# Mixing stage of the first block: the short tile of sparse attention moved into the first long tile, the second long tile turned over two PSUM banks

## The chip, the cores and the metric

The kernel runs on one core of one Trainium2 chip. The metric is the device time of one execution in microseconds (us); lower is better. The median of three runs is 3070.9 us (3065.38 to 3075.09).

## What is computed

A first block of two layers over 272 tokens (16 meta tokens and 256 of the sequence) of width 1024, then a second block of two layers. The change is in the first block. Each of its layers begins with one projection of the tokens and two mixers on its columns:

```
proj = h @ w_in[l]
dq, dk, dv, dz, db, da, sq, sk, sv, iq, ik, iw = split(proj)
o_dn = deltanet_group(dq, dk, dv, dz, db, da, ...)        # gated delta rule, 4 heads
o_sa = dsa_group(sq, sk, sv, iq, ik, iw, ..., k_top=64)   # sparse attention, 8 heads of 64
mix  = concatenate([o_dn, o_sa]) @ w_out[l]
```

In the sparse attention an index score (Relu of 8 products of iq and ik, weighted by iw) picks the 64 best earlier tokens of each token; the attention is a softmax over those alone:

```
score  = sum_h relu(qi . ki / 8) * wi ;  sel = top_k(score, 64)
logits = q . k[sel] / 8, masked where sel > position
out    = softmax(logits) @ v[sel]
```

The first 16 tokens have no more than 16 earlier ones, so all are taken and no ranking is needed.

## The kernel before

The 272 tokens lie in three tiles, TILES = (0, 16), (16, 128), (144, 128); below they are the short, the first long and the second long tile, c = 0, 1, 2. The mixing stage (mixers) has three parts that share the engines: projections (35 products n = 0 to 34, each of 16 TensorE instructions, most of 128 x 272), delta_rule and sparse_attention. Each part gives each engine a generator. A generator yields a due time and then issues the instructions of one step; together() always takes the generator with the smallest due time. The due times are plain numbers without a unit that the engine sees: they fix the order in which an engine's instructions are put, once, when the program is built, and nothing more. An engine works through that order and stops at any semaphore that is not yet there.

The steps that matter here:

- projection_time(n): due time of projection n. Projections 0 to 11 feed the convolution of the delta rule, 12 to 14 its gates, 15 the index key (ik), 16 to 19 iq, 20 to 23 sq, 24 to 27 sk, 28 to 30 the values sv (7 us each), 31 to 34 the output gate z. Results are copied out of PSUM by ScalarE (L267 to L276). A rotated copy for the rope goes through four DMAs (swap, L206), then VectorE (L311 to L316).
- on_tensor of projections first turns the layer's parameters (L224), which six small loads bring (L168), and then starts projection 0 (L247), which waits for three loads made ahead (load_ahead, L119).
- Ranking, RANK_START: for each long tile and head an index product (L707) on TensorE, a Relu (L757) on ScalarE and an accumulation (L802, L804) on VectorE, with two banks and two buffers, so that product h waits for Relu h-2 and Relu h for accumulation h-2. Then eight rounds of maximum and replace (L814, L816).
- Attention, ATTEND_ORDER = (1, 2, 0) at ATTEND_START = (116, 157, 198): logits (L724) head by head, scaled and masked by VectorE (L838), row maximum (L841), exponential (L766), reciprocal (L847), scaling (L773). Then for each head: turn of the probabilities into bank 6 (L735), copy to SBUF in one instruction for each of the c + 1 key tiles (L783), product with the values (L743). At the end of a tile one copy into mixT (L787).
- The delta rule goes over the three tiles too: steps gcum/gc, kv, kk, LA, then levels v with products LX (L450), YP (L457) and PY (L460) and subtractions on VectorE (L645, L648), then wu (L465, L467), wS (L474) and oS (L479 to L482). At due time 177 it closes with squares (L508), a product with ones (L408), logarithms (L511) and an exponential (L513).
- mix_and_route follows: its first product (L991) reads all of mixT.

Of the kernel before, what the change touches and what calls it, by code (L numbers as in the profile page):

```python
# [9 lines left out]
ALU = mybir.AluOpType  # L10
# [3 lines left out]
P = 128  # L14
# [119 lines left out]

def projections(nc, m, l, A, S):
# [196 lines left out]
def delta_rule(nc, m, S, ctx):  # L332
# [182 lines left out]
    def chunk_on_scalar(act, c, t0, n):  # L515
# [23 lines left out]
        if c == 2:  # L539
            yield end_time(c, 4)  # L540
# [124 lines left out]
RANK_START = {1: 80.0, 2: 98.0}  # L665
ATTEND_ORDER = (1, 2, 0)
ATTEND_START = (116.0, 157.0, 198.0)


def sparse_attention(nc, m, S, ctx):  # L670
# [12 lines left out]
    den = sb("s_den", [P, NH])  # L683

# [4 lines left out]
    RANKED = [t0 + n > TOP_K for t0, n in TILES]  # L689
    assert RANKED == [False, True, True]  # L690

    def half(h):
        return slice(64 * (h % 2), 64 * (h % 2) + 64)

    def on_tensor(pe):
# [13 lines left out]
        for a, c in enumerate(ATTEND_ORDER):  # L709
            t0, n = TILES[c]  # L710
            ns = t0 + n
            at = ATTEND_START[a]
            for h in range(NH):
# [5 lines left out]
                if h < 2 and a:  # L719
                    pe.wait_ge(S["s_pT_sb"], a * NH)  # L720
                    pe.wait_ge(S["s_out"], a)
                if h >= 2:
                    pe.wait_ge(S["s_logit_sb"], q - 1)
                nc.tensor.matmul(ps[6 + h % 2][0:n, 0:ns], m.sqT[half(h), h // 2, t0:t0 + n], m.skT[half(h), h // 2, 0:ns],  # L724
                                 start=True, stop=True).then_inc(S["s_logit"], 1)
            for h in range(NH):
# [4 lines left out]
                if h:  # L731
                    pe.wait_ge(S["s_pT_sb"], q)
                for j in range(c + 1):
                    s0, w = TILES[j]
                    mm = nc.tensor.transpose(ps[6][0:w, j * P:j * P + n], lg[0:n, h, s0:s0 + w], m.ident[0:n, 0:n])  # L735
                mm.then_inc(S["s_pT"], 1)
                yield at + 24.5 + 2.2 * h
                if q == 0:
                    pe.wait_ge(S["proj_by_act"], 12 + 13 + 3)
                pe.wait_ge(S["s_pT_sb"], q + 1)  # L740
# [6 lines left out]
    def on_scalar(act):  # L747
# [10 lines left out]
        for a, c in enumerate(ATTEND_ORDER):  # L758
            t0, n = TILES[c]
            ns = t0 + n  # L760
            at = ATTEND_START[a]
# [2088 lines left out]
```

## Time and profile before

| | |
|---|---|
| median of 3 runs | 3070.9 us (3065.38 to 3075.09) |
| profiled execution, its time | 3067.97 us |
| its span, first to last instruction | 3065.9 us |
| TensorE busy, matmuls | 2507.4 us, 82% of the span |
| VectorE busy | 856.7 us, 28% |
| ScalarE busy | 572.3 us, 19% |
| TensorE clock granted, mean | 0.878 |

The span is 2.1 us shorter than the profiled execution's own time. Rows of the trace are read as follows. PE is TensorE's matmuls, PEld its weight loads, DVE VectorE, ACT ScalarE, SPq the queue that issues the DMAs. A row of the timeline has the start, the duration, the engine, the line of the kernel, the operation with its result and its inputs, the shape and how many instructions are merged in it; in brackets how long the engine was idle before it and what ended that. A row of the windows has the stretch and its length, then busy time and count for PE, PEld, DVE, ACT and POOL, then the granted TensorE clock (1.00 is 2.4 GHz, 0.50 is 1.2 GHz), the share of the DMA engines' time and GB/s. A row of the groups has busy time and mean duration in ns, then the idle time before. Both layers run the same instructions; rows of the first stand for both where nothing else is said.

### The profile page before, as it was taken

What the parts mean: (1) busy time and instruction counts of PE and PEld (TensorE: products, weight loads), DVE (VectorE), ACT (ScalarE), POOL (GpSimd) and SP (SyncE); (2) the same over time, 40 slices, a digit from 0 to 9 for tenths busy, and PEclk for the clock granted to TensorE, in tenths of its full rate; (3) what the DMA queues carried; (4) which work ended last, traced back from release to release, by engine and by line L of the source; (5) the groups of instructions that cost most, each with busy time, mean ns of one, the idle gap of its engine ahead of it and who ended that gap; (6) DMA issues with size and microseconds to landing.
All of it is one profiled execution on the core that took longest, in us unless ns stands there. A gap on an engine that the chain in (4) does not pass through costs nothing. (4 is left out here: it accounts for less than half of the span.)

```text
span 3065.9 us, 32692 instructions
## 1 busy us (share of the span) xinstructions
PE 2507.4 (82%) x12088; PEld 1844.6 (60%) x12088; DVE 856.7 (28%) x2016; ACT 572.3 (19%) x1323; POOL 0.2 (0%) x4
## 2 busy tenths in 40 slices
PE   6888768786989668874787888989979778798998
PEld 5665544335766454432655567778867556687886
DVE  2472043223473042223112352111110324411111
ACT  1214120102213210012112222011010223301110
POOL 0000000000000000000000000000000000000000
PEclk9999769998889669997898688999989868899999
DMA  5120319992220218993633002533244220233331
GB/s 184 65 70 28 136 41 396 399 393 79 85 70 28 110 55 336 408 399 128 183 117 110 1 1 83 184 118 137 109 112 154 64 82 1 77 116 137 137 137 41
DMA packets 162921, 422.16 MB, mean 138 GB/s; under 512 B 40306, under 2 KB 54108, under 8 KB 138220
## 3 DMA queue, kind: packets, MB, share of 16 engines
q1 hardware_dynamic: 162796, 420.56, 37.4%
q8 instruction: 71, 1.16, 0.2%
q14 instruction: 54, 0.44, 0.0%
HBM read 414.82 MB, written 1.05 MB: 136 GB/s over the span
## 5 line engine op out<-in xcount | busy, mean ns | idle before, releaser
L2611 PE MATMUL bank<-hT,W 128*128 128x256 f32 x1024 | 229.5, 385 | 19.1 <-DVE hT L1603 11.9
L2619 PE MATMUL bank<-u_hid,W 128*128 128x256 f32 x1024 | 225.2, 381 | 19.2 <-ACTq L2633 19.2
L247 PE MATMUL bank<-hT,W 128*128 128x272 f32 x928 | 237.8, 414 | 0.0
L2611 PEld LDWEIGHTS bank<-hT,W 128*128 128x128 f32 x1024 | 196.2, 193 | 52.3 <-issue 25.4
L2619 PEld LDWEIGHTS bank<-u_hid,W 128*128 128x128 f32 x1024 | 193.2, 190 | 51.1 <-issue 25.5
L247 PEld LDWEIGHTS bank<-hT,W 128*128 128x128 f32 x928 | 184.9, 202 | 44.0 <-issue 4.3
L1230 PE MATMUL bank<-W,e_hs 128*32 128x512 f32 x1024 | 138.4, 701 | 60.2 <-DMA W<-in_w 58.5
L2644 DVE TENSOR_TENSOR xT<-xT,bank 128x256 f32<-128x256 f32 x128 | 53.9, 421 | 428.7 <-PE bank L2619 428.7
L1209 PE MATMUL bank<-e_sel,rowsH 128*128 128x128 f32 (+1 forms) x768 | 149.2, 328 | 19.3 <-DVEq L1317 11.6
L1209 PEld LDWEIGHTS bank<-e_sel,rowsH 128*128 128x128 f32 (+1 forms) x768 | 113.9, 204 | 62.8 <-issue 25.3
L2521 PE MATMUL bank<-hT,W 128*128 128x256 f32 x512 | 122.1, 394 | 20.0 <-PEq L2473 18.3
L1230 PEld LDWEIGHTS bank<-W,e_hs 128*32 128x32 f32 x1024 | 40.4, 126 | 157.0 <-issue 157.0
L2521 PEld LDWEIGHTS bank<-hT,W 128*128 128x128 f32 x512 | 101.0, 199 | 38.5 <-issue 23.8
L1772 PE MATMUL bank<-hT,W 128*128 128x256 f32 (+1 forms) x544 | 121.9, 384 | 2.3 <-issue 2.1
L1772 PEld LDWEIGHTS bank<-hT,W 128*128 128x128 f32 (+1 forms) x544 | 99.8, 185 | 24.0 <-issue 8.9
L2630 ACT ACTIVATE u_rel<-bank 128x256 f32<-128x256 f32 x64 | 24.5, 383 | 402.1 <-PE bank L2611 402.1
L1220 PE MATMUL bank<-e_back,e_y 128*128 128x272 f32 x288 | 83.7, 413 | 18.9 <-DVE yT L1336 13.1
L2434 PE MATMUL bank<-hT,W 128*128 128x256 f32 x256 | 77.7, 470 | 3.5 <-DVEq L2454 3.5
L1220 PEld LDWEIGHTS bank<-e_back,e_y 128*128 128x128 f32 x288 | 45.6, 188 | 52.7 <-DVE yT L1336 45.1
L2434 PEld LDWEIGHTS bank<-hT,W 128*128 128x128 f32 x256 | 60.8, 244 | 18.1 <-DVEq L2454 3.9
L1336 DVE TENSOR_TENSOR yT<-yT,bank 128x272 f32<-128x272 f32 x144 | 61.6, 437 | 33.6 <-PE bank L1220 29.6
L991 PE MATMUL bank<-mixT,W 128*128 128x272 f32 x256 | 64.9, 418 | 1.7 <-PEq L875 1.1
(535 smaller groups left out, 3332.5 us busy)
## 6 DMA issues: line engine op xcount, KB each, us to landing
W<-in_w SPq DMA_DIRECT2D x128, 1024.0 KB, 10.2
W<-in_w_in SPq DMA_DIRECT2D x41, 2048.0 KB, 9.0
e_Wd<-in_w SPq DMA_DIRECT2D x64, 1024.0 KB, 10.3
W<-in_w_up SPq DMA_DIRECT2D x16, 2048.0 KB, 9.0
W<-in_w_down SPq DMA_DIRECT2D x16, 2048.0 KB, 7.9
W<-in_w_out SPq DMA_DIRECT2D x8, 2048.0 KB, 8.4
W<-in_cmp_w SPq DMA_DIRECT2D x4, 2048.0 KB, 8.7
W<-in_mem_w_kv SPq DMA_DIRECT2D x4, 2048.0 KB, 8.1
```

Source lines behind the costliest of these rows:

```text
L247: mm = nc.tensor.matmul(bank[:, 0:T], w[:, k, c0:c0 + P], m.hT[:, k, :], **st)
L991: mm = nc.tensor.matmul(ps[n % 4][:, 0:T], w[:, k, n % 4 * P:n % 4 * P + P], m.mixT[:, k, :], start=(k == 0), stop=(k == KT - 1))
L1209: mm = nc.tensor.matmul(o, m.rowsH[0:nt, c, d * P:(d + 1) * P], sel[0:nt, c, :], start=(c == 0), stop=(c == 2))
L1220: nc.tensor.matmul(ps[6 + d % 2][:, 0:T], y[:, d * P:(d + 1) * P], back[:, 0, :], start=True, stop=True).then_inc(S["e_part"], 1)
L1230: mm = nc.tensor.matmul(ps[2][32 * j:32 * j + 32, :], hs[:, k, 32 * j:32 * j + 32], Wu[:, j, :, k, :], start=(k == 0), stop=(k == KT - 1))
L1336: nc.vector.tensor_tensor(m.yT[:, d, :], m.yT[:, d, :], ps[6 + d % 2][:, 0:T], ALU.add).then_inc(S["e_y_free"], 1)
L1772: mm = nc.tensor.matmul(o, wv[:, k, a:a + w], m.hT[:, k, :], **st)
L2434: mm = nc.tensor.matmul(bank[:, 0:S2], wm[:, k, n % 4 * P:n % 4 * P + P], m.hT[:, k, :], start=(k == 0), stop=(k == KT - 1))
L2521: mm = nc.tensor.matmul(ps[q % 2][:, 0:S2], wm[:, k, n % 4 * P:n % 4 * P + P], m.hT[:, k, :], start=(k == 0), stop=(k == KT - 1))
L2611: mm = nc.tensor.matmul(ps[j % 2][:, 0:S2], wa[:, k, j * P:(j + 1) * P], m.hT[:, k, :], start=(k == 0), stop=(k == KT - 1))
L2619: mm = nc.tensor.matmul(ps[4 + n % 2][:, 0:S2], wb[:, k, n * P:(n + 1) * P], hid[:, x, k, :], start=(k == 0), stop=(k == 3))
L2644: nc.vector.tensor_tensor(m.xT[:, n, :], m.xT[:, n, :], ps[4 + n % 2][:, 0:S2], ALU.add).then_inc(S["u_y_free"], 1)
```

## The change

1. The short tile leaves the third place of ATTEND_ORDER. Its work for all eight heads is done in one piece inside the first long tile: logits into banks 6 and 7 after that tile's logits, mask, maximum and subtraction on VectorE, one exponential on ScalarE, sum and division on VectorE, eight turns into bank 6, one copy, eight products, one copy into mixT.
2. The second long tile turns its heads alternately into banks 6 and 0.
3. A head's copies out of the turn bank (one for each key tile) become one instruction over all key tiles and all 128 partitions.
4. The turn of the parameters goes behind projections 0 and 1.
5. Due times: projections 20 and up, RANK_START of the second long tile 98 to 92, ATTEND_START 116 to 120 and 157 to 161, the gate's Silu.

```diff
@@ projection_time
+    if n < 20:
+        return 54.0 + 4.0 * (n - 15)
     if n < 28:
-        return 54.0 + 4.0 * (n - 15)
+        return 75.0 + 5.0 * (n - 20)
     if n < 31:
-        return 112.0 + 12.0 * (n - 28)
-    return 148.0 + 5.0 * (n - 31)
+        return 122.0 + 8.0 * (n - 28)
+    return 146.0 + 6.0 * (n - 31)
@@ projections, on_tensor
-        yield 0
-        pe.wait_ge(S["params_loaded"], 16 * 6)
-        nc.tensor.transpose(ps[7][:, 0:81], m.prm[0:81, :], m.ident[0:81, 0:81]).then_inc(S["params_turned"], 1)
...
         for n, (kind, chunk, c0, idx) in enumerate(plan):
+            if n == 2:
+                pe.wait_ge(S["params_loaded"], 16 * 6)
+                nc.tensor.transpose(ps[7][:, 0:81], m.prm[0:81, :], m.ident[0:81, 0:81]).then_inc(S["params_turned"], 1)
@@ delta_rule, chunk_on_scalar
-            yield end_time(c, 4)
+            yield max(end_time(c, 4), projection_time(34) + 4)
@@ sparse_attention
-RANK_START = {1: 80.0, 2: 98.0}
-ATTEND_ORDER = (1, 2, 0)
-ATTEND_START = (116.0, 157.0, 198.0)
+RANK_START = {1: 80.0, 2: 92.0}
+ATTEND_START = {1: 120.0, 2: 161.0}
...
+    def turn_bank(a, h):
+
+        return ps[0] if a and h % 2 else ps[6]
@@ sparse_attention, on_tensor
+            if a == 0:
+                yield at + 9.5
+                pe.wait_ge(S["s_logit_sb"], NH)
+                for h in range(NH):
+                    mm = nc.tensor.matmul(ps[6 + h % 2][0:M, h // 2 * M:h // 2 * M + M], m.sqT[half(h), h // 2, 0:M], m.skT[half(h), h // 2, 0:M], start=True, stop=True)
+                mm.then_inc(S["s_short_logit"], 1)
+                yield at + 17
+                pe.wait_ge(S["s_short_prob"], 1)
+                for h in range(NH):
+                    mm = nc.tensor.transpose(ps[6][0:M, M * h:M * h + M], short[:, 0, h, :], m.ident[0:M, 0:M])
+                mm.then_inc(S["s_short_pT"], 1)
+                yield at + 19
+                pe.wait_ge(S["proj_by_act"], 12 + 13 + 1)
+                pe.wait_ge(S["s_short_pT_sb"], 1)
+                for h in range(NH):
+                    mm = nc.tensor.matmul(ps[7][half(h), h // 2 * M:h // 2 * M + M], m.sv[0:M, 0, h * 64:(h + 1) * 64], short[:, 1, h, :], start=True, stop=True)
+                mm.then_inc(S["s_short_pv"], 1)
             for h in range(NH):
                 q = a * NH + h
                 yield at + 23 + 2.2 * h
                 if h == 0:
                     pe.wait_ge(S["s_prob"], a + 1)
-                if h:
+                if a == 0 and h:
                     pe.wait_ge(S["s_pT_sb"], q)
+                if a and h == 1:
+                    pe.wait_ge(S["proj_by_act"], 12 + 13 + 3 + 4)
+                if a and h >= 2:
+                    pe.wait_ge(S["s_pT_sb"], q - 1)
                 for j in range(c + 1):
                     s0, w = TILES[j]
-                    mm = nc.tensor.transpose(ps[6][0:w, j * P:j * P + n], lg[0:n, h, s0:s0 + w], m.ident[0:n, 0:n])
+                    mm = nc.tensor.transpose(turn_bank(a, h)[0:w, j * P:j * P + n], lg[0:n, h, s0:s0 + w], m.ident[0:n, 0:n])
                 mm.then_inc(S["s_pT"], 1)
                 yield at + 24.5 + 2.2 * h
@@ sparse_attention, on_scalar
+                if a == 0 and h == 4:
+                    act.wait_ge(S["s_short_in"], 1)
+                    nc.scalar.activation(short[:, 0, :, :], short[:, 0, :, :], ACT.Exp).then_inc(S["s_short_exp"], 1)
...
-                for j in range(c + 1):
-                    w = TILES[j][1]
-                    i = nc.scalar.activation(pT[0:w, h % 2, j, 0:n], ps[6][0:w, j * P:j * P + n], ACT.Copy)
-                i.then_inc(S["s_pT_sb"], 1)
-            yield at + 41.5
+                nc.scalar.activation(pT[:, h % 2, 0:c + 1, 0:n], turn_bank(a, h)[:, 0:(c + 1) * P].rearrange("p (j t) -> p j t", j=c + 1)[:, :, 0:n],
+                                     ACT.Copy).then_inc(S["s_pT_sb"], 1)
+            yield at + 42
```

On ScalarE the copy of the turned probabilities of the short tile stands behind scaling 1 of the first long tile and its copy into mixT behind scaling 6. On VectorE the short tile's mask and maximum are due at 132, its sum and division at 135.5, both between steps of the first long tile.

## Rows read from the trace of the kernel before

**Rows 1.** The page, part 1: busy time, share of the span, instructions.

```profile
PE 2507.4 (82%) x12088; PEld 1844.6 (60%) x12088; DVE 856.7 (28%) x2016; ACT 572.3 (19%) x1323; POOL 0.2 (0%) x4
```

**Rows 2.** The windows, whole core, three of the first layer's.

```profile
160.00:190.00 30.00, 28.11 (x158) 21.91 (x156) 23.40 (x52) 6.54 (x17) 0.00 (x0) 1.00 0.13 47
...
205.00:220.00 15.00, 8.88 (x46) 7.06 (x46) 11.22 (x31) 1.19 (x2) 0.00 (x0) 0.77 0.00 0
...
333.00:347.00 14.00, 5.40 (x41) 3.78 (x39) 1.66 (x12) 5.73 (x33) 0.00 (x0) 0.50 0.00 0
```

**Rows 3.** The timeline, end of the first layer's mixing stage.

```profile
306.93 0.81 PE L735 MATMUL bank<-k_ident,W 128*16 128x128 f32 x3 [4.71 <-ACTq L774]
307.77 0.58 ACT L783 ACTIVATE W<-bank 16x128 f32<-16x128 f32 x3 [0.92 <-PE bank L735]
...
308.40 1.73 PE L743 MATMUL bank<-W,sv 16*64 16x128 f32 x6 [0.67 <-ACT W L783]
...
332.13 0.60 ACT L787 ACTIVATE mixT<-bank 128x512 f32<-128x512 f32 x1 [1.81 <-PE bank L743]
...
346.89 17.10 PE L991 MATMUL bank<-mixT,W 128*128 128x272 f32 x64 [0.57 <-PEq L875]
...
364.25 14.91 PE L991 MATMUL bank<-mixT,W 128*128 128x272 f32 x64 [0.26 <-issue]
```

**Rows 4.** The groups by shape, 306 to 333 us.

```profile
L783 ACT ACTIVATE W<-bank 128x128 f32<-128x128 f32 x16 | 3.2, 249 | 0.0
```

**Rows 5.** The timeline from the last delta product to the scalings.

```profile
290.37 1.06 PE L482 MATMUL bank<-d,d 128*128 128x128 f32 x8
...
292.40 0.51 ACT L766 ACTIVATE W<-W,s_mx 128x272 f32<-128x272 f32 x1
...
297.69 1.37 ACT L508 ACTIVATE d_sq<-d_oT 128x272 f32<-128x272 f32 x4
...
304.09 1.11 ACT L513 ACTIVATE d_sq<-d_sq 128x1088 f32<-128x1088 f32 x1
...
305.11 1.74 ACT L773 ACTIVATE W<-W,s_den 128x272 f32<-128x272 f32 x4
```

**Rows 6.** The timeline and DMA issues, start of both layers' stages.

```profile
12.29 4.94 SPq L119 DMA_DIRECT2D W<-in_w_in  x1
...
32.68 0.40 PE L224 MATMUL bank<-k_ident,prm 81*128 81x81 f32 x1 [10.31 <-DMA prm<-in_ln_b]
...
W<-in_w_in SPq DMA_DIRECT2D x1, 2048.0 KB, 19.8
...
725.30 0.07 DVE L1502 MEMSET xT<- 128x9 f32 x1 [11.92 <-issue]
...
728.67 0.40 PE L224 MATMUL bank<-k_ident,prm 81*128 81x81 f32 x1 [23.35 <-DMA prm<-in_ln_b]
```

**Rows 7.** The timeline, ranking and delta levels, engine by engine.

```profile
156.51 5.62 PE L247 MATMUL bank<-hT,W 128*128 128x272 f32 x16
...
194.50 7.04 PE L242 MATMUL bank<-W,hT 128*16 128x512 f32 x16
...
211.98 0.84 PE L724 MATMUL bank<-skT,sqT 64*128 64x144 f32 x2 [5.14 <-DVE W L838]
...
229.84 1.95 PE L450 MATMUL bank<-d,d 128*128 128x128 f32 x16
...
163.06 0.69 DVE L645 TENSOR_TENSOR d<-d,bank 128x512 f32<-128x512 f32 x1 [4.12 <-PE bank L457]
...
179.78 0.36 DVE L802 TENSOR_SCALAR s_score<-W,bai 128x272 f32<-128x272 f32 x1
...
180.26 0.40 ACT L757 ACTIVATE W<-bank 128x272 f32<-128x272 f32 x1 [4.79 <-DVEq L805]
...
119.79 2.41 SPq L206 DMA_DIRECT2D xT<-iqT  x4
...
124.60 1.29 DVE L311 TENSOR_TENSOR xT<-xT,k_sin 128x1088 f32<-128x1088 f32 x1 [0.89 <-DMA xT<-iqT]
```

More of the change, by code:

```diff
@@ L683, in sparse_attention @@
     den = sb("s_den", [P, NH])
+    M = N_META
+    short = sb("s_short", [M, 2, NH, M])
+    short_bias = sb("s_short_bias", [M, M])
+    short_mx = sb("s_short_mx", [M, 2, NH])
     room, at = m.W[:, SLOTS - 1, :], NH * T
@@ L688, in sparse_attention @@
     pT = room[:, at + 2 * T:at + 2 * T + 6 * P].rearrange("p (h j t) -> p h j t", h=2, j=3)
-    RANKED = [t0 + n > TOP_K for t0, n in TILES]
-    assert RANKED == [False, True, True]
+    assert TILES[0] == (0, M) and M <= TOP_K
     def half(h):
         return slice(64 * (h % 2), 64 * (h % 2) + 64)
+    def turn_bank(a, h):
+        return ps[0] if a and h % 2 else ps[6]
     def on_tensor(pe):
@@ L708, in on_tensor @@
                                  start=True, stop=True).then_inc(S["s_idx"], 1)
-        for a, c in enumerate(ATTEND_ORDER):
+        for c in (1, 2):
             t0, n = TILES[c]
             ns = t0 + n
-            at = ATTEND_START[a]
+            at = ATTEND_START[c]
+            a = c - 1
             for h in range(NH):
@@ L739, in on_tensor @@
                     pe.wait_ge(S["proj_by_act"], 12 + 13 + 3)
+                    pe.wait_ge(S["s_short_out"], 1)
                 pe.wait_ge(S["s_pT_sb"], q + 1)
@@ L757, in on_scalar @@
                 nc.scalar.activation(rel[0:n, h % 2, 0:ns], ps[6 + h % 2][0:n, 0:ns], ACT.Relu, scale=0.125).then_inc(S["s_rel"], 1)
-        for a, c in enumerate(ATTEND_ORDER):
+        for c in (1, 2):
             t0, n = TILES[c]
             ns = t0 + n
-            at = ATTEND_START[a]
+            at = ATTEND_START[c]
+            a = c - 1
             yield at + 11
@@ L773, in on_scalar @@
                 nc.scalar.activation(lg[0:n, h, 0:ns], lg[0:n, h, 0:ns], ACT.Copy, scale=den[0:n, h:h + 1])
+                if a == 0 and h == 1:
+                    act.wait_ge(S["s_short_pT"], 1)
+                    nc.scalar.activation(short[:, 1, :, :], ps[6][0:M, 0:NH * M].rearrange("s (h t) -> s h t", h=NH), ACT.Copy).then_inc(S["s_short_pT_sb"], 1)
+                if a == 0 and h == 6:
+                    act.wait_ge(S["s_short_pv"], 1)
+                    nc.scalar.activation(m.mixT[:, 4:8, 0:M], ps[7][:, 0:4 * M].rearrange("p (h t) -> p h t", h=4), ACT.Copy).then_inc(S["s_short_out"], 1)
             act.drain().then_inc(S["s_prob"], 1)
@@ L822, in on_vector @@
             dve.drain()
-        for a, c in enumerate(ATTEND_ORDER):
+        yield ATTEND_START[1] - 1
+        nc.vector.tensor_scalar(short_bias[:, :], m.causal[0:M, 0, 0:M], -1.0, BIG, ALU.add, ALU.mult)
+        dve.drain()
+        for c in (1, 2):
             t0, n = TILES[c]
             ns = t0 + n
-            at = ATTEND_START[a]
-            mask = bias[0:n, c - 1 if RANKED[c] else 0, 0:ns]
-            if not RANKED[c]:
-                yield at
-                nc.vector.tensor_scalar(mask, m.causal[0:n, c, 0:ns], -1.0, BIG, ALU.add, ALU.mult)
-                dve.drain()
+            at = ATTEND_START[c]
+            a = c - 1
+            mask = bias[0:n, a, 0:ns]
             for h in range(NH):
@@ L844, in on_vector @@
             dve.drain().then_inc(S["s_max"], 1)
+            if a == 0:
+                yield at + 12
+                dve.wait_ge(S["s_short_logit"], 1)
+                w = short[:, 0, :, :]
+                for y in range(2):
+                    nc.vector.scalar_tensor_tensor(w[:, y:NH:2, :], ps[6 + y][0:M, 0:NH // 2 * M].rearrange("s (h t) -> s h t", h=NH // 2), 0.125,
+                                                   short_bias[:, :].unsqueeze(1).to_broadcast([M, NH // 2, M]), ALU.mult, ALU.add)
+                dve.drain()
+                nc.vector.tensor_reduce(short_mx[:, 0, :], w, AX.X, ALU.max)
+                dve.drain()
+                nc.vector.tensor_tensor(w, w, short_mx[:, 0, :].unsqueeze(2).to_broadcast([M, NH, M]), ALU.subtract)
+                dve.drain().then_inc(S["s_short_in"], 1)
+                yield at + 15.5
+                dve.wait_ge(S["s_short_exp"], 1)
+                nc.vector.tensor_reduce(short_mx[:, 1, :], w, AX.X, ALU.add)
+                dve.drain()
+                nc.vector.reciprocal(short_mx[:, 1, :], short_mx[:, 1, :])
+                dve.drain()
+                nc.vector.tensor_tensor(w, w, short_mx[:, 1, :].unsqueeze(2).to_broadcast([M, NH, M]), ALU.mult)
+                dve.drain().then_inc(S["s_short_prob"], 1)
             yield at + 17
```

13 lines of the change are left out of this document (7 added, 6 removed).

## The prediction

> **What bounds the kernel now.** The page's first part says TensorE is busy for 82% of the span [rows 1]. That average hides the stage this change is in: the mixing stage, which runs once a layer, from 32.7 to 346.9 us and again from 728.7 us. The windows show its two halves. The first is crowded: from 160 to 190 us TensorE is busy 28.1 of 30 us at full clock, and the hole is from 205 to 220 us, 8.9 busy of 15 us at a granted clock of 0.77. The end is a chain with little beside it: from 333 to 347 us TensorE is busy 5.4 of 14 us at a granted clock of 0.50, which is 1.2 GHz [rows 2]. The timeline of that end shows the second long tile's eight heads one after another from 306.93 us to the tile's output copy at 332.13 us, 3.15 us each, then the short tile alone, and only at 346.89 us the output projection (L991), which needs all of mixT [rows 3]. So I read the change as: take the short tile off the end, and pay for it in the crowded part.
>
> **The end of the stage: what is removed.** The second tile's output copy ends at 332.73 us and L991 starts at 346.89 us [rows 3]. No more of that than the 0.57 us that L991's row has as idle before it is the handover, which stays. I take 13.8 us as gone in each of the two layers (bounds 13.6 and 14.2).
>
> **The turns over two banks.** One head costs 0.84 us to the first copy, 0.58 us of copies, 0.05 us of wait, and the rest of its 3.15 us, 1.7 us, is products; TensorE idles 0.67 us for the copies [rows 3]. The diff lets head h+1 turn into the other bank, but TensorE takes its instructions in the order they were put: turn h, product h, turn h+1. Product h still waits for copy h, and turn h+1 is behind it. The second bank removes no wait; I cost it at nothing. What does shrink is the copy, three instructions into one of 384 columns. A copy of 128 columns takes 0.249 us [rows 4] and one of 512 takes 0.60 us [rows 3]. On the line between them 384 take 0.48 us: 0.10 us less a head, 0.8 us a layer. Its bounds are 0 and 1.6 us (a strided read as slow as three copies, or all but the 0.25 us and its columns overlapped). The Trainium skill (PSUM — Partial Sum Buffer, Summary: rules for kernel authors) says to aim a read of PSUM at another bank than the running matmul's; that rule would credit the second bank with the 0.67 us. It has its place below as a rival.
>
> **How the end begins.** Due times decide each engine's order, and ATTEND_START of the second tile goes from 157 to 161 while the delta rule's end stays at 177. On ScalarE the last exponential and all eight scalings now fall behind the delta rule's closing squares, logarithms and exponential, where before four scalings were ahead. Before: the last delta product ends at 291.4 us, the first turn starts at 306.93 us, 15.5 us later; squares to exponential take 7.5 us (297.69 to 305.2), four scalings 1.74 us, an exponential 0.51 us [rows 3, 5]. After: the row maximum now ends with the last delta product; seven exponentials and the state's copy take 4.3 us, the closing block 7.5, the last exponential, the reciprocal and eight scalings 4.7 with their handovers, together 16.5 us: 1.0 us later (bounds 0 and 2).
>
> **How it starts.** The transposed parameters move behind two projections. In layer 0 TensorE started at 32.68 us, but the third load ahead, issued at 12.29 us, landed 19.8 us later, at 32.1 us: 0.6 us gained (bounds 0 and 0.6). In layer 1 the weights had long landed and TensorE waited for the parameters until 728.67 us, while VectorE was in the stage at 725.30 us: 3.4 us gained (bounds 2.4 and 3.4) [rows 6]. The turn of the parameters, now behind the second projection, has the convolution waiting for it instead; two projections of 3.7 us cover the loads.
>
> **The crowded part.** Projections 20 to 27 become due later, the ranking of the second long tile earlier (98 to 92). I merged the due times and gave each step its duration before.
> - Index products 1 to 7 of the first tile lose projections 22 and 23 as filler. The delta rule's product wu waits about 2.3 us for VectorE. Projection 23 ends at about 161.0 us; before, everything up to there with projection 24 too had ended at 162.0, and a projection costs 3.7 us (64 such instructions 14.91 us, a projection has 16) [rows 3, 7]. Lag: 2.7 us.
> - Now the second tile's index products stand in front of projection 25. That of head 4 waits for a Relu that waits for VectorE's first accumulation of this tile. Before, ScalarE already idled 4.79 us at this Relu, under TensorE's filler. VectorE got from 163.06 us to that accumulation at 179.78 us without rest; the same list, less a 1.4 us rope addition that moves behind it, takes 15.7 us to its end. It also gets a wait: the rotated copy now is queued on ScalarE behind the decay exponentials, and 4.8 us from issue to use (119.79 to 124.60 us) bring it at 173 us, 3.2 us after VectorE wants it [rows 7]. So head 4 can go at 181 us, and TensorE is through with the rest at 171: it waits 10 us, with projections 25, 26, 27 and the second tile's delta steps behind it.
> - Then VectorE is the bound to the first tile's logits, with TensorE waiting again for 2.7, 4.0 and 1.0 us; the old wait of 5.14 us at 211.98 us goes. TensorE has then still the 7.0 us product sv0, which before filled the busy time ahead. All logits and delta level 5 are done at about 233.5 us; before, that with another 7.0 us product (sv1) was done at 229.84 us [rows 7], so 222.9 without. Lag: 10.6 us, of which 3 us is the half clock after waits. Bounds 5 and 15.
> - The short tile's work on TensorE is 5.4 us at 0.50 [rows 2], 2.7 us at full clock, and this part is TensorE's: 2.7 us. Its softmax on VectorE and ScalarE lies beside sv1's 7 us, but its last step waits for ScalarE, where a delta copy is ahead: 1.0 us on TensorE. Without sv1 as cover it would cost some 4 us.
> - In the first tile's head loop six heads instead of three have no filler between turn and product: 3 times 0.5 us, 1.6 us with the rounding. The second tile's logits save 0.5 us.
>
> **Sum.** Layer 0: 10.6 + 2.7 + 1.0 + 1.6 - 0.5 + 1.0 = 16.4 us paid; 13.8 + 0.8 + 0.6 = 15.2 gained: 1.2 us slower. Layer 1: 16.4 paid, 18.0 gained: 1.6 us faster. Together -0.4 us on the profiled 3068.0 us; the median is 2.9 us above that, so 3070 us.
>
> **Rivals.**
> - *The ranking's wait is mostly made up (faster).* The old hole (5.14 us and the half clock after it) could go and the new one be half of mine. For it: VectorE's work is the same and begins earlier. Against it: the order is fixed, and the head 4 product cannot pass. At a lag of 0 to 5 us the two layers give 11 to 21 us: 3049 to 3059 us. It decides below a lag of 6 us.
> - *The clock (slower).* Four waits in place of one. L991 after the idle end ran 17.10 us for 64 instructions and 14.91 us for the next 64 [rows 3], 2.2 us for each restart. I counted 3 us; two more restarts a layer, and one microsecond on VectorE's chain behind each, give 2 x 6.4 = 13 us: 3083 us. It decides from about 4.6 us a layer. The Trainium skill (TensorE: Matmul & The Clock Gate, What's actually happening) has the slow clock as the default that activity lifts; the 0.77 of 205 to 220 us agrees [rows 2].
> - *Two banks do overlap.* If turn h+1 ran under copy h, 0.67 us would go for seven heads a layer: 9.4 us, 3061 us. Against it stands the order of instructions, plainly.
>
> **Numbers.** What this kernel's measurement can tell is about 0.3%, 9 us. No measurable change, my forecast, 0.42 (own range 3061 to 3080 us); the made-up wait 0.30; overlap 0.03; the clock and longer chains 0.25. Faster by more than 0.3%: 0.33; within: 0.42; slower: 0.25. Range for 8 in 10: 3047 to 3085 us.
>
> **What would show it.** Right: L991 follows the second tile's output copy at once; heads of that tile 3.0 us apart with the 0.6 us idle kept; a TensorE wait of 8 to 12 us at L707 (after, its moved line) with the clock at half behind it; the second layer's start 3.4 us nearer to its barrier. Wrong: no such wait, or turn-to-turn at 2.5 us; then the end's gain comes through and the kernel is about 1% faster. Wrong the other way: the part before the last delta product longer by over 20 us.

## The result, and the profile after

The changed kernel takes 3081.1 us (median of 17, 3070.2 to 3093.7 without one execution of 10347.55 us that the comparison leaves out) against 3069.8 us (17, 3061.6 to 3075.1): ratio 1.0037, 95% interval 1.0025 to 1.0050, slower by more than the 0.3% that I had called the limit. The time is in the range and the sign is wrong: the forecast was no change at 3070 us, and the time is that of the rival "the clock (slower)", 3083 us. Whether its mechanism came too is taken up below. The profiled execution took 3083.2 us, its span is 3081.1 us.

Page, part 1, of the changed kernel (compare [rows 1]):

```profile
PE 2517.9 (82%) x12088; PEld 1850.5 (60%) x12088; DVE 855.9 (28%) x2008; ACT 560.1 (18%) x1215; POOL 0.2 (0%) x4
```

The same number of matmuls takes 10.5 us more. By the windows, 6.7 us of this lie in code that the diff does not touch (286.7 us of matmuls for 284.2 between the first output projection and the barrier, 1678.1 for 1674.0 from the second output projection to the end), so only 3.8 us belong to the two mixing stages. Three windows of the first layer follow; the first two have the bounds of [rows 2], the third lies at about the same distance from the output projection:

```profile
160.00:190.00 30.00, 21.14 (x97) 15.68 (x96) 18.86 (x45) 5.14 (x14) 0.00 (x0) 0.80 0.28 89
205.00:220.00 15.00, 9.39 (x42) 8.44 (x42) 12.91 (x29) 1.59 (x3) 0.00 (x0) 0.66 0.38 109
339.00:353.00 14.00, 10.88 (x40) 6.24 (x40) 0.00 (x0) 2.56 (x5) 0.00 (x0) 0.50 0.00 0
```

The end is dense now (10.9 us of matmuls for 5.4), but 160 to 190 us, which was full, has 97 matmuls for 158. Over the whole crowded part, first before and then after:

```profile
120.00:240.00 120.00, 108.05 (x591) 79.63 (x590) 78.00 (x164) 23.91 (x70) 0.00 (x0) 0.91 0.21 67
```

```profile
120.00:240.00 120.00, 97.76 (x528) 74.99 (x527) 71.97 (x155) 16.16 (x43) 0.00 (x0) 0.83 0.21 66
```

TensorE idles 10.3 us more in the same 120 us, at a granted clock of 0.83 for 0.91. The timeline of the crowded part after the change:

```profile
142.65 6.60 PE L249 MATMUL bank<-hT,W 128*128 128x272 f32 x16
...
157.56 5.98 PE L249 MATMUL bank<-hT,W 128*128 128x272 f32 x16
...
182.87 0.40 ACT L788 ACTIVATE W<-bank 128x272 f32<-128x272 f32 x1 [11.66 <-DVEq L844]
183.32 3.03 PE L715 MATMUL bank<-ikT,iqT 64*128 64x272 f32 x6 [8.12 <-ACT W L788]
186.28 2.07 PE L459 MATMUL bank<-d,d 128*128 128x128 f32 x8
...
209.60 2.08 PE L452 MATMUL bank<-d,d 128*128 128x128 f32 x8 [2.77 <-DVEq L636]
...
214.51 2.08 PE L452 MATMUL bank<-d,d 128*128 128x128 f32 x8 [2.83 <-DVEq L648]
...
223.54 0.52 PE L733 MATMUL bank<-skT,sqT 64*128 64x144 f32 x4 [0.92 <-DVEq L319]
...
237.80 0.51 PE L733 MATMUL bank<-skT,sqT 64*128 64x144 f32 x2
...
239.33 0.37 PE L739 MATMUL bank<-skT,sqT 64*16 64x16 f32 x16
...
251.27 0.35 PE L744 MATMUL bank<-k_ident,s_short 16*16 16x16 f32 x8 [0.94 <-DVEq L903]
...
259.88 0.64 PE L750 MATMUL bank<-s_short,sv 16*64 16x16 f32 x16
```

L715 is the index product, L788 its Relu, L733 the long tiles' logits, L739, L744 and L750 the short tile's logits, turn and product. The wait that I had put in front of the index product of head 4 is there with its releaser, ScalarE's Relu behind VectorE's accumulation; what stands behind it, and both projections above, run in part at half clock (6.60 and 5.98 us; 3.83 at full). The end of the stage:

```profile
327.76 0.81 PE L765 MATMUL bank<-k_ident,W 128*16 128x128 f32 x3 [7.29 <-ACTq L815]
328.61 0.49 ACT L822 ACTIVATE W<-bank 128x384 f32<-128x384 f32 x1 [0.92 <-PE bank L765]
329.15 1.73 PE L774 MATMUL bank<-W,sv 16*64 16x128 f32 x6 [0.58 <-ACT W L822]
330.81 0.81 PE L765 MATMUL bank<-k_ident,W 128*16 128x128 f32 x3
...
352.24 0.60 ACT L826 ACTIVATE mixT<-bank 128x512 f32<-128x512 f32 x1 [1.82 <-PE bank L774]
353.15 16.46 PE L1050 MATMUL bank<-mixT,W 128*128 128x272 f32 x64 [0.94 <-PEq L934]
```

The output projection (L1050) follows the tile's output copy at once, 25.4 us behind the first turn for 40.0 before [rows 3]; heads are 3.05 us apart for 3.15. The second layer starts 0.95 us behind its barrier for 3.4 [rows 6]:

```profile
735.31 0.07 DVE L1562 MEMSET xT<- 128x9 f32 x1 [12.23 <-issue]
...
736.26 9.04 PE L249 MATMUL bank<-hT,W 128*128 128x272 f32 x26 [21.25 <-issue]
```

**Where the 15.2 us of span are.** The first layer's stage ends 6.3 us later (346.89 to 353.15). The second layer's stage, from its barrier's memset to its output projection, takes 325.7 us for 323.0: +2.7. The remaining 6.2 us are in code that the diff does not touch: +3.8 between the first output projection and the barrier, +2.5 from the second output projection to the end. The last section has what these are. So below I read experiments by two numbers: the ratio, and the *stage sum*, which is the start of the first layer's output projection plus the second layer's time from memset to output projection: 669.9 us before, 678.9 us after. The medians are 11.3 us apart, the two profiled executions 15.2.

### The profile page after: what moved, and what is told of

Read it like the earlier page. It is cut to its first block and busy times, and to the rows that moved or that the text cites. A ratio compares the mean times of both kernels' runs of the same rounds, so it can differ in the third digit from the quotient of the medians.

```text
span 3081.1 us, 32572 instructions
## 1 busy us (share of the span) xinstructions
PE 2517.9 (82%) x12088; PEld 1850.5 (60%) x12088; DVE 855.9 (28%) x2008; ACT 560.1 (18%) x1215; POOL 0.2 (0%) x4
## 3 DMA queue, kind: packets, MB, share of 16 engines
q8 instruction: 71, 1.16, 0.2%
## 5 line engine op out<-in xcount | busy, mean ns | idle before, releaser
L249 PEld LDWEIGHTS bank<-hT,W 128*128 128x128 f32 x928 | 185.9, 203 | 76.4 <-issue 25.4
L1268 PE MATMUL bank<-e_sel,rowsH 128*128 128x128 f32 (+1 forms) x768 | 149.2, 328 | 19.4 <-DVEq L1376 11.6
L1268 PEld LDWEIGHTS bank<-e_sel,rowsH 128*128 128x128 f32 (+1 forms) x768 | 113.9, 204 | 62.8 <-issue 25.4
L1832 PEld LDWEIGHTS bank<-hT,W 128*128 128x128 f32 (+1 forms) x544 | 100.3, 186 | 25.3 <-issue 11.3
L1279 PE MATMUL bank<-e_back,e_y 128*128 128x272 f32 x288 | 83.7, 413 | 18.9 <-DVE yT L1395 13.1
L1050 PE MATMUL bank<-mixT,W 128*128 128x272 f32 x256 | 63.8, 413 | 2.4 <-PEq L934 1.9
## 6 DMA issues: line engine op xcount, KB each, us to landing
e_Wd<-in_w SPq DMA_DIRECT2D x64, 1024.0 KB, 10.3
```

The lines of the kernel that those rows point to most:

```text
L249: mm = nc.tensor.matmul(bank[:, 0:T], w[:, k, c0:c0 + P], m.hT[:, k, :], **st)
L1050: mm = nc.tensor.matmul(ps[n % 4][:, 0:T], w[:, k, n % 4 * P:n % 4 * P + P], m.mixT[:, k, :], start=(k == 0), stop=(k == KT - 1))
L1268: mm = nc.tensor.matmul(o, m.rowsH[0:nt, c, d * P:(d + 1) * P], sel[0:nt, c, :], start=(c == 0), stop=(c == 2))
L1279: nc.tensor.matmul(ps[6 + d % 2][:, 0:T], y[:, d * P:(d + 1) * P], back[:, 0, :], start=True, stop=True).then_inc(S["e_part"], 1)
L1832: mm = nc.tensor.matmul(o, wv[:, k, a:a + w], m.hT[:, k, :], **st)
```

## Experiments

Sixteen kernels were run. All ratios are to the kernel before, in runs on the same chip. The chip was not the same for all (the kernel before took 3067.2 to 3071.0 us in the medians), so between two experiments the ratios compare better than the times.

**1. The due times alone.** *olddue* is the changed kernel with the old due times (only the gate's Silu keeps its new rule):

```diff
-RANK_START = {1: 80.0, 2: 92.0}
-ATTEND_START = {1: 120.0, 2: 161.0}
+RANK_START = {1: 80.0, 2: 98.0}
+ATTEND_START = {1: 116.0, 2: 157.0}
```

and projection_time as before. *newdue* is the kernel before with the new ones (its short tile at 202).

> The changed kernel with the due times of the kernel before (projections, RANK_START 98, ATTEND_START 116 and 157); short tile, banks, merged copy and late parameter turn stay. Theory 1 (the new due times cost: ranking ahead of the projections opens an 8.1 us TensorE wait and half clock behind it, 15.3 us a layer to the first long tile's last logits): the part up to the last delta product goes back to within 5 us of before, the end keeps its 14.6 us, stage end of layer 0 near 336 us, whole kernel 3041 to 3049 us. Rival (the short tile's work in the crowded part costs what it saves at the end): no less than 3068 us.

> The kernel before with the new due times alone (short tile still at the end, due at 202). Theory 1: about 16 us a layer slower, 3095 to 3105 us, with the 8 us wait at the index product of head 4 of the second long tile. Rival: within 9 us of before.

*olddue*: 3045.6 us, ratio 0.9927 (0.9910 to 0.9944), stage sum 642.0. *newdue*: 3102.1 us, 1.0107 (1.0090 to 1.0124), 707.5. The new due times cost 35.5 us in the changed kernel and 32.4 us in the old one; everything else in the diff together gains 24. Both times are in the range of Theory 1. In *olddue* the same index product waits 0.86 us:

```profile
187.67 0.72 PE L713 MATMUL bank<-ikT,iqT 64*128 64x272 f32 x2 [0.86 <-ACT W L786]
...
203.66 0.52 PE L731 MATMUL bank<-skT,sqT 64*128 64x144 f32 x4
```

and the first logits go at 203.7 us for 223.5.

**2. Which of the three due times.** With the projections' old times: *oldproj* (index 92, attention 120), *rank92* (index 92, attention 116), *attend120* (index 98, attention 120). With the projections' new times: *rank98* (index 98, attention 120). The edit is in each case one or two of the lines above.

> The changed kernel with RANK_START of the second long tile back to 98, its projection times kept. Theory 1 in its narrow form (the ranking's earlier start alone is the cost): the 8 us wait at head 4 goes, 3055 to 3063 us. If it is the projections' later times that matter (rope and sv0 late), the time stays within 5 us of 3081 us.

> The changed kernel with the due times of the projections as before the change, and the new due times of the index products (92) and of the attention (120 and 161). With all the old due times it took 3045.6; with only the index products' old due time 3072.2. Theory A (what costs is that rope and sv projections stand later in TensorE's order, behind the second part of the delta rule): 3044 to 3056, with the first projections to the output at 333 to 341 us in the first layer. Theory B (what costs is the index products' early place, which puts a wait for VectorE's score steps into TensorE's order; the late projections only add to it): the 8 us wait in front of the index product of head 4 is still there and the time is 3062 to 3075.

> The changed kernel with the old due times of the projections and of the index products (98), and the new ones of the attention (120 and 161 for 116 and 157). All three old: 3045.6, the first long tile's last logit product at 218.3 us. The index products' alone old: 3072.2 and 237.2 us. The projections' alone old: 3066.7 and 236.8 us. Each of these two alone leaves the logits 18 us late; only together are they undone, unless it is the attention's 120 that does it, which both runs kept. Theory A (the two due times together; the attention's does nothing by itself): the last logit at 218 to 222 us and 3044 to 3052. Theory B (the attention's later due time holds a stretch of the delta rule ahead of the logits, and is the cause): 230 us or later, and 3060 or more.

> The changed kernel with the old due times of the projections and of the attention (116 and 157), and the new one of the index products (92 for 98). With the attention at 120 this took 3066.7, with an 7.8 us wait in front of the second pair of index products for ScalarE's Relu, which waits for VectorE's score steps, and a second wait of 6.0 us for VectorE. Theory A (the index products' early place is what costs, whatever the attention's due time): 3060 to 3070 and both waits still there. Theory B (the attention's due time of 120 is what costs): 3044 to 3052.

| projections | index | attention | kernel | time, us | ratio (interval) | stage sum | last logit of the first long tile |
|---|---|---|---|---|---|---|---|
| old | 98 | 116 | olddue | 3045.6 | 0.9927 (0.9910 to 0.9944) | 642.0 | 218.3 |
| old | 98 | 120 | attend120 | 3052.2 | 0.9950 (0.9937 to 0.9963) | 655.8 | 234.8 |
| old | 92 | 116 | rank92 | 3058.9 | 0.9971 (0.9961 to 0.9982) | 658.5 | 228.2 |
| old | 92 | 120 | oldproj | 3066.7 | 0.9989 (0.9979 to 1.0000) | 664.1 | 236.8 |
| new | 98 | 120 | rank98 | 3072.2 | 1.0011 (0.9999 to 1.0022) | 672.0 | 237.2 |
| new | 92 | 120 | after | 3081.1 | 1.0037 (1.0025 to 1.0050) | 678.9 | 237.8 |

The attention's and the index products' times cost by themselves; the projections' new times were run only with the attention at 120, and cost there. In stage sums the attention's later start costs 13.8 us with the index products at 98 and 5.6 at 92, the early index products 6.9 to 16.5, the projections' new times 14.8 to 16.2. So neither *oldproj* (Theory B's time) nor *rank98*, which gave back 9 us, undid the loss alone. *rank98* came out between its two theories: the wait at the index product shrinks from 8.1 to 2.7 us, and another for VectorE takes its place:

```profile
217.43 2.07 PE L452 MATMUL bank<-d,d 128*128 128x128 f32 x8 [6.78 <-DVEq L648]
```

In *rank92* the waits of Theory A are there, at a time 1 us under its range. For *attend120* neither theory held: its time is at A's upper end and its last logit is 16 us later than in *olddue*, as B asked, while the stage ends only 9.1 us later in the first layer. So a logit's time is no measure of the stage. Each of these due times moves a wait for VectorE into TensorE's order: in *attend120* and *rank92*

```profile
217.21 2.08 PE L450 MATMUL bank<-d,d 128*128 128x128 f32 x8 [6.18 <-DVEq L646]
```

```profile
182.03 1.27 PE L713 MATMUL bank<-ikT,iqT 64*128 64x272 f32 x2 [7.77 <-ACT W L786]
...
208.82 2.08 PE L450 MATMUL bank<-d,d 128*128 128x128 f32 x8 [5.98 <-DVEq L634]
```

**3. The parts that were to gain.** *start* is the kernel before with the late turn of the parameters alone; *noshort* the changed kernel without the short tile's work (it leaves out that tile's attention and fills its 16 columns of the mixing output from elsewhere, so that only the stage can be compared); *onebank* the changed kernel with `return ps[6]` in turn_bank and the old waits; *overlap* issues the next head's turn ahead of this head's product in the second long tile (turn(h) is the changed kernel's turn with its waits):

```diff
             for h in range(NH):
                 q = a * NH + h
                 yield at + 23 + 2.2 * h
+                if a == 0 or h == 0:
+                    turn(h)
+                if a and h + 1 < NH:
+                    turn(h + 1)
```

> The kernel before with one part of the change alone: the turn of the parameters stands behind two projections instead of ahead of the first. By the changed kernel's trace the second layer's first projection starts 0.95 us behind the barrier instead of 3.37; the first layer's is held by its weights' transfer either way and gains at most the 0.9 us of the turn. Theory A (the gain at the start is passed on to the end of the stage): 3069.7 - 2.4 - 0.5 = 3066.8, range 3065.5 to 3068. Theory B (the chain through VectorE and the transfers' landing hold the rest, so that the start's gain is lost): 3069 to 3070.5.

> The changed kernel without any of the 16-token tile's work (logits, softmax, turn and product; its 16 columns of the mixing output are filled from another tile by one copy at the place of the output's copy, so the routing of those 16 tokens differs and only the mixing stage is to be compared). By the changed kernel's trace the tile's instructions hold TensorE for about 1.2 us and one wait of 0.9 a layer, and the head loop's waits grew by 1.9 with the longer ScalarE queue. Theory A: the stretch from the first long tile's last logit to the last delta product (73.6 us in the changed kernel, 68.6 before) gets 3 to 4.5 us shorter. Theory B (the tile is hidden, and the 5 us come from the due times and the clock): it gets less than 1.5 us shorter. The stretch up to the first long tile's last logit (237.8 us) stays within 1 us in either.

> The changed kernel with the turns of the second long tile in one bank, each waiting for the copy of the head before, as before the change. In the changed kernel each head's turn stands behind the product of the head before, which itself waits for that head's copy, so the second bank lets nothing start earlier: heads 3.05 us apart, the idle time ahead of each product 0.58. Theory A (the second bank by itself gives nothing): the same 3.05 us and 3081, range 3078 to 3084. Theory B (it hides the part of the copy's wait that stands ahead of the turn): heads 3.3 us or more apart, 3084 to 3088.

> The changed kernel with the second long tile's turn of head h+1 put before the product of head h, so that the second bank is used. Theory 2 (in the changed kernel the two banks do nothing, by the order): the 0.58 us of TensorE idle at each product goes for seven heads, 4 us a layer, 3072 to 3075 us. Rival (the end is bound by ScalarE or by the banks, the order does not matter): 3081 us, heads still 3.05 us apart.

*start*: 3066.2 us, ratio 0.9983 (0.9972 to 0.9994), stage sum 667.0: the gain at the start arrives. The sum hides 2.0 us lost in the first layer and 4.9 gained in the second.

*noshort*: 3070.7 us. From the last logit product of the first long tile to the first of the norm's products it takes 75.96 us in both layers, for 78.7 and 80.3 with the tile: the tile costs 2.8 and 4.3 us: Theory A, in the first layer a little under its 3 us.

*onebank*: 3082.6 us, ratio 1.0043 (1.0030 to 1.0056), stage sum 682.9; the 4.0 over the changed kernel are not at its edit but in the crowded part of the second layer (212.1 us from memset to the first long tile's last logit, for 208.8), so a stage sum is good to some 4 us. *overlap* gains more than the 3072 to 3075 us that its expectation had. The heads of *onebank* and those of *overlap* (3067.3 us, ratio 0.9988, 0.9976 to 1.0001, stage sum 669.0):

```profile
328.48 0.81 PE L761 MATMUL bank<-k_ident,W 128*16 128x128 f32 x3 [7.29 <-ACTq L811]
329.86 1.73 PE L770 MATMUL bank<-W,sv 16*64 16x128 f32 x6 [0.58 <-ACT W L818]
331.52 0.81 PE L761 MATMUL bank<-k_ident,W 128*16 128x128 f32 x3
```

```profile
331.24 1.73 PE L781 MATMUL bank<-W,sv 16*64 16x128 f32 x6
332.90 0.81 PE L764 MATMUL bank<-k_ident,W 128*16 128x128 f32 x3
333.64 1.73 PE L781 MATMUL bank<-W,sv 16*64 16x128 f32 x6
```

One bank: 3.04 us apart, the same 0.58 us idle ahead of each product, 25.4 us from the first turn to the output projection, as with two. Two banks and the turn ahead of the product: 2.40 us apart, no idle time, 20.1 us. The Trainium skill (PSUM — Partial Sum Buffer, Summary: rules for kernel authors) asks that a read go to another bank than the running matmul's. By these rows that gives nothing while the matmuls' order makes each wait for the read, and 5.3 us a layer once the order allows it.

**4. Is the half clock a cost of its own?** *fill17* puts products that nobody reads into the 8.1 us wait, *fillearly* also 6 and 8 into the waits at 133 and 138 us:

```diff
+                if q == 12:
+                    pe.wait_ge(S["proj_by_act"], 12 + 9)
+                    for _ in range(17):
+                        nc.tensor.matmul(ps[1][:, 0:T], m.ident[:, :], m.hT[:, 0, :], start=True, stop=True)
```

> The changed kernel with 17 products of 128 x 272 that nobody reads (into a bank that is free there) in front of the index product of head 4, where TensorE stands for 8.1 us in every layer of the changed kernel's trace. In that trace the granted clock is 0.50 from 180 to 188 us, and the six index products and the first YP and P products behind the wait take 3.03 + 2.07 + 1.49 us, against about 1.5 + 1.05 + 1.05 at full clock. Theory A (the wait costs twice, once as idle time that other engines spend anyway and once as half clock behind it): the wait shrinks to under 1 us, what stands behind it runs at full clock and ends 2 to 3 us earlier; but VectorE's chain, which TensorE then waits for, takes part of it back, so 1 to 2.5 us a layer, 3076 to 3080 against the changed kernel's 3081. Theory B (the half clock is only a companion of the wait, the chain through VectorE sets the time): 3080 to 3083. Theory C: the dummy products last longer than the wait and delay the rest: up to 3090.

> The changed kernel with the 17 unread products of fill17 and 14 more: 6 ahead of the first index product (a wait of 1.4 us at 133 us) and 8 ahead of the short delta tile's last step (a wait of 2.0 us at 138 us). In the changed kernel's trace the granted clock is 0.50 from 136 to 144 us and 0.74 from 144 to 152, and there stand two steps of 1.88 us and a projection of 6.60 us that take 1.06 and 3.83 at full clock; VectorE is busy for only 2.5 of the 8 us, so nothing but TensorE sets the pace there. fill17 alone took the stage from 330.6 to 329.2 us between the first projection and the output projection in the mean of the layers. Theory A (the half clock at 136 to 150 us is a cost of its own, of some 4 us a layer by these rows): the stage ends 2.5 to 5 us earlier a layer than in fill17, 3065 to 3071 against its 3075.7. Theory B (what TensorE gains there it waits for VectorE in the crowded part, 170 to 220 us, where VectorE is busy for 7 of 8 us): less than 1.5 us a layer, 3073 to 3077.

*fill17*: 3075.7 us, ratio 1.0009 (0.9998 to 1.0019), stage sum 677.4. *fillearly*: 3082.4 us, 1.0043 (1.0029 to 1.0057), 678.7. First *fill17*, then *fillearly*:

```profile
177.65 7.96 PE L716 MATMUL bank<-hT,k_ident 128*128 128x272 f32 x34
185.92 1.34 PE L719 MATMUL bank<-ikT,iqT 64*128 64x272 f32 x4 [0.31 <-ACT W L792]
...
188.23 1.16 PE L459 MATMUL bank<-d,d 128*128 128x128 f32 x8
```

```profile
174.68 7.96 PE L723 MATMUL bank<-hT,k_ident 128*128 128x272 f32 x34
183.85 1.34 PE L726 MATMUL bank<-ikT,iqT 64*128 64x272 f32 x4 [1.22 <-ACT W L799]
...
186.72 2.08 PE L459 MATMUL bank<-d,d 128*128 128x128 f32 x8
```

In *fill17* the step behind the wait is at full clock (1.16 us for 2.07). From projection 23 to the last logit it takes 77.1 us for the changed kernel's 80.2 us. Of these 3.1 us, 0.7 is that projection's own time (5.31 for 5.98), ahead of the fill. And it began 3.3 us later, so the stage gained only 0.4 and 1.0 us, while the median is 5.4 us under the changed kernel's, just below the range of Theory A (3076 to 3080): stages and times do not tell the same. In *fillearly* a product shows as two records of 0.24 us; 14 of them last 7 us in waits of 3.4, a slip of mine. They held the clock at 1.00 from 128 to 144 us, but projection 23 began at 157.16 us all the same, for 157.56, so they spent what that gave; behind the 1.2 us that were left of the long wait, the step was at half clock again. Its time lies above both of its ranges, and with its slip it decides nothing on the early half clock. So filling the long wait is worth 0.4 to 2.4 us a layer by the traces, and what the clock costs in the end stays open.

**5. A faster version.** *best* is *olddue* with *overlap*'s order. *bestfill* and *bestfill10* add 18 and 10 unread products ahead of the logit product of head 2, where TensorE waits 5.4 us; *beforefill10* puts 10 into the same wait of the kernel before [rows 7].

> The changed kernel with all due times as before the change (3045.6) and with the next head's turn ahead of this head's product in the second long tile, where the two banks allow it. In the changed kernel that reordering made the heads 2.40 us apart instead of 3.05 and the stage from the first turn to the output projection 20.1 us instead of 25.4, 5.3 us a layer, and the time 3067.3 instead of 3081. If the two gains add, 3045.6 - 10.6 = 3035, range 3031 to 3039. Rival: an earlier end of the mixing stage meets weights that are not loaded yet, and part of the gain is lost in a wait of the output projection or of the experts for a transfer: 3038 to 3046.

> The kernel called best (3042.7 us) with 18 unread products ahead of the logit product of head 2, where TensorE stands for 5.4 us in every layer because VectorE is at the last ranking steps; behind the wait six logit products and two steps of eight products take 2.5 + 3.6 us at half clock in its trace against some 1.6 + 2.1 at full clock. Theory A (the clock behind the wait is a cost): 1.5 to 2.5 us a layer, 3037 to 3041. Theory B (VectorE's own chain covers it, as it did in the stage of fill17): 3041 to 3045.

> The kernel called bestfill (3030.8 us) with 10 unread products for 18. In bestfill's trace each of them shows as two records of 0.23 us, so that 18 last 8.4 us, 2 us longer than the wait that they fill (6.4 us from the last product before to the logit product in the kernel called best); 10 last 4.7 us and leave 1.2 to 1.7 us of it. In bestfill the stretch from the first to the last logit product of the first long tile is 14.95 us in both layers, in best 14.66 and 15.27. Theory A (the clock behind the wait is what it costs, and 18 products gave part of it back by their own length): the stretch takes 13 to 13.7 us, each layer's stage ends 1 to 2 us earlier than bestfill's, 3026 to 3031. Theory B (what bestfill gained over best did not come from this wait but from the clock in parts whose code is the same, 10.3 of its 14.6 us of span): the stretch stays within 0.5 us of 14.95 and the time is anywhere in 3030 to 3043.

> The kernel before the change with the same 10 unread products in its own wait of 5.1 us ahead of the logit product of head 2. Theory A: the stretch from the first to the last logit product of the first long tile, 14.5 and 15.0 us in its two layers, takes 13 to 13.7 us, and the time is 3064 to 3068 against 3069. Theory B: 3068 to 3070.

| kernel | time, us | ratio (interval) | stage sum | first to last logit, two layers |
|---|---|---|---|---|
| best | 3042.7 | 0.9911 (0.9893 to 0.9928) | 634.3 | 14.66, 15.27 |
| bestfill | 3030.8 | 0.9878 (0.9854 to 0.9901) | 629.8 | 14.95, 14.95 |
| bestfill10 | 3031.4 | 0.9894 (0.9878 to 0.9911) | 632.0 | 14.31, 14.31 |
| beforefill10 | 3067.8 | 1.0006 (0.9996 to 1.0016) | 672.4 | 14.07, 14.12 |

In *best* and then *bestfill10*:

```profile
212.02 0.85 PE L731 MATMUL bank<-skT,sqT 64*128 64x144 f32 x2 [5.36 <-DVE W L882]
213.85 0.84 PE L731 MATMUL bank<-skT,sqT 64*128 64x144 f32 x2 [0.98 <-DVE W L882]
```

```profile
210.38 4.75 PE L732 MATMUL bank<-hT,k_ident 128*128 128x272 f32 x20
215.91 0.51 PE L735 MATMUL bank<-skT,sqT 64*128 64x144 f32 x2 [0.78 <-DVE W L886]
217.73 0.51 PE L735 MATMUL bank<-skT,sqT 64*128 64x144 f32 x2 [1.32 <-DVE W L886]
```

The logit products halve, but the next waits for VectorE anyway, 0.3 us longer than before. Filling this wait takes 0.4 to 1 us off the stretch and nothing measurable off the kernel before. That is nearer to Theory B in both, but *bestfill10*'s stretch is 0.6 us off B's 14.95 and *beforefill10*'s time is at the edge of A's range. *bestfill* is 6 us below the lowest of its ranges and yet its stretch did not get shorter (14.95 for 14.66 and 15.27), so that gain is not from this wait. The three fast versions, 0.9 to 1.2% under the kernel before, cannot be told apart surely; that *olddue* and *overlap* add holds for the stages (642.0 to 634.3: 7.7 of 10.6 expected) and not for the times (3045.6 to 3042.7). *best*'s time is that of the rival in its expectation, but the rival's cause, a wait behind the stage for late weights, does not show: from the first output projection to the barrier it takes 383.4 us for *olddue*'s 383.6, and of the 8.5 us more from the second one to the end 5.2 are longer matmuls (last section).

## Why the prediction was wrong

- **The end of the stage: right.** 14.6 us gone from the first turn to the output projection; I had 13.8 + 0.8.
- **Two banks: right.** Costed at nothing; 3.05 us with two banks, 3.04 with one. The merged copy takes 0.49 us for 0.58, and the heads are 0.10 us closer, as the line between two rows had given.
- **How the end begins: nearly.** First turn 15.9 us behind the last delta product for 15.5: +0.4, I had +1.0.
- **The start: right in kind.** 2.4 us gained in the second layer, the lower of my bounds; I had taken the upper, 3.4. In the first layer the first projection starts at 32.54 us for 32.87: 0.3 of my 0.6.
- **The short tile's work: right in sum.** Its rows hold TensorE 1.4 us (I had 2.7), its turn waits 0.94 us (1.0). From the last logit to the last delta product the changed kernel takes 73.6 us for 68.6, +5.0; I had 2.7 + 1.0 + 1.6 - 0.5 = 4.8. *noshort* puts 2.8 and 4.3 us of it to the tile.
- **The crowded part: the step that failed, by its size.** I wrote "All logits and delta level 5 are done at about 233.5 us" and "Lag: 10.6 us". They were done at 238.2, for 229.8 less 7.0 before: 15.4 us. The waits were there, one by one: 8.1, 2.8, 2.8 and 0.9 us where I had 10, 2.7, 4.0 and 1.0. What was wrong is the lag that I made of them. The windows from the stage's first TensorE instruction to that point have the same matmuls but for the 16 of sv1 (7.13 and 7.56 us), which only the kernel before has there; first before, both layers, then after:

```profile
32.68:229.84 197.16, 180.98 (x934) 138.01 (x935) 110.42 (x252) 46.43 (x120) 0.00 (x0) 0.93 0.25 77
728.67:931.44 202.77, 187.74 (x934) 143.91 (x935) 110.39 (x252) 46.54 (x120) 0.00 (x0) 0.89 0.24 76
```

```profile
32.54:238.24 205.70, 179.88 (x917) 139.97 (x918) 108.16 (x249) 43.57 (x107) 0.00 (x0) 0.88 0.24 74
736.26:944.54 208.28, 182.82 (x917) 142.77 (x917) 108.17 (x249) 43.58 (x107) 0.00 (x0) 0.86 0.24 74
```

| | first layer | second layer | I had |
|---|---|---|---|
| TensorE idles longer | 9.6 | 10.4 | 7.6 |
| the same matmuls take longer | 6.0 | 2.6 | 3.0 |
| the stretch is longer | 15.7 | 13.1 | 10.6 |

The 15.7 is the 15.4 with 7.13 us for sv1 and a start 0.1 us earlier. The counts after the change are one below 934 less 16: a record is missing. My 7.6 us are the 10.6 less the 3.0.

So the idle time was too small in both layers, and the half clock, "of which 3 us is the half clock after waits", in the first alone. The 7.6 us of idle time did not follow from my own waits: 17.7 us, and the 2.3 us at the product wu, less the 7.9 that the old kernel waits there (5.14 and three of 0.9 to 1.0) are 12.1.

- **How the half clock got into the lag.** It was there before the long wait too. I had given projections 22 and 23 their durations before,

```profile
137.13 5.19 PE L247 MATMUL bank<-hT,W 128*128 128x272 f32 x16
...
145.10 3.93 PE L247 MATMUL bank<-hT,W 128*128 128x272 f32 x16
```

and they took 6.60 and 5.98: 3.5 us more, and 23 ended 2.5 us after my 161.0. VectorE's chain to the head 4 product starts behind the step after it, at 164.97 us for 163.06, and takes 17.8 us for my 18.9; so the product went at 183.3 for my 181. Behind it, six index products and the step after them took 5.1 us, some 2.4 more than at full clock (half of the 3.03, and 1.16 for the step as in *fill17*). The steps are read from the rows; no experiment removes the half clock alone, and the filled waits give back only a part of it.

- **Added up.** By the steps: 15.4 + 5.0 + 0.4 - 14.6 = 6.2 us in the first layer, where the stage end is 6.3 us late and I had 1.2. The second came out at +2.7 for my -1.6: 2.5 us more in the crowded part, 1.0 less gained at the start, and 0.9 less behind. The due times cost 36.9 us of stage sum against *olddue*, 18.4 a layer, where my terms for them (10.6 and 1.0) made 11.6.
- **The rivals.** "The clock" had the time, and set its turning point at 4.6 us a layer; the miss was 5.1 and 4.3. Its mechanism is a part: matmuls 3.0 us longer than I counted in the first layer and none in the second, where it had 4.4 us of restarts in each. So its time came in part by luck. "The made-up wait" fell with the 8.1 us. "Two banks do overlap" needed an order the diff does not have; with it, it holds.

## What to carry to other kernels

Where the order on every engine is fixed by due times, price the due times apart from the work that they make room for: here the work moved gained 24 us and the new times gave 35 back. When work is taken out of a full stretch to go elsewhere, the durations in it are no longer those of the old trace, on either side of a new wait; and a lag has to add up: idle time gained and lost, plus what the same instructions take longer. A second buffer is worth nothing until the instruction that would use it is issued ahead of the wait that it is to hide.

## What the runs showed of the hardware

Code that no edit touches takes different times. The windows from the first output projection to the barrier and from the second output projection to the end, in *best* and then in *olddue*:

```profile
329.80:713.20 383.40, 290.83 (x1626) 167.67 (x1626) 116.31 (x344) 45.28 (x79) 0.00 (x0) 0.85 0.69 279
1017.60:3038.50 2020.90, 1677.23 (x7644) 1272.45 (x7644) 467.59 (x1065) 342.69 (x721) 0.00 (x0) 0.88 0.37 134
```

```profile
334.60:718.20 383.60, 289.06 (x1626) 166.46 (x1626) 116.32 (x344) 45.30 (x79) 0.00 (x0) 0.85 0.69 279
1025.60:3038.00 2012.40, 1672.07 (x7644) 1269.57 (x7644) 467.62 (x1065) 342.71 (x721) 0.00 (x0) 0.88 0.37 135
```

7644 matmuls both times, VectorE and ScalarE busy to 0.03 us alike, and 8.5 us between them, of which TensorE's busy time is 5.2. Over all the profiles the long stretch took 2012.4 to 2020.9 us and the other 378.3 to 384.9. So 6.2 of the changed kernel's 15.2 us, and the 3 us by which *best* is under *olddue*, are within what unchanged code varies. The Trainium skill (TensorE: Matmul & The Clock Gate, Part 1) says that the clock's rise is variable from run to run; the busy times agree, and what it adds up to here is the number above.
